# Keeping the residual feature-major in a two-block transformer kernel on one Trainium2 core

## The reference, cut to what matters

```
def rmsnorm(x, g):  xf * rsqrt(mean(xf*xf, -1) + EPS) * g
x = x + mixed @ w_out                      # block 1: three branches: gated delta rule, forget attention, stick breaking
x = x + mem_attn(rmsnorm(x, norm_xq), rmsnorm(mem, norm_mem)) @ w_mo
x = x + (silu(conv(h @ w_up)[a]) * conv(h @ w_up)[b]) @ w_down       # h = rmsnorm(x, norm_ffn)
x = x + 0.5 * rmsnorm(swiglu(rmsnorm(x, ffn1_pre)), ffn1_post)       # block 2
x = x + rmsnorm([moba attention, pooling](rmsnorm(x, mix_pre)) @ w_out_2, mix_post)
x = x + rmsnorm(xa_attn(rmsnorm(x, xa_pre), rmsnorm(mem_2, mem_g)) @ xa_wo, xa_post)
x = x + 0.5 * rmsnorm(swiglu(rmsnorm(x, ffn2_pre)), ffn2_post)
```

## Time and profile before

| | us |
|---|---|
| median of three runs | 1322.25 (1321.5 to 1328.23) |
| the profiled execution, first to last instruction | 1314.1 |
| TensorE busy | 1214.3 (92%) |
| VectorE busy | 722.1 (55%) |
| ScalarE busy | 631.5 (48%) |
| first feed-forward up projections | 503.7 to 631.2 |
| second | 700.6 to 828.1 |
| third | 1118.15 to 1245.3 |

### The profile page before, as it was taken

How to read it: one execution, slowest core, us unless ns; L and a number is a source line. 1 busy time by engine, 2 the same in 40 slices (tenths; PEclk the granted TensorE clock), 3 DMA queues, 4 the chain that set the end, 5 groups by cost and what they waited for, 6 DMA issues and landing times. The chain is left out here.

```text
span 1314.1 us, 19389 instructions
## 1 busy us (share of the span) xinstructions
PE 1214.3 (92%) x8179; PEld 1112.4 (85%) x8179; DVE 722.1 (55%) x797; ACT 631.5 (48%) x785; POOL 51.1 (4%) x81
## 2 busy tenths in 40 slices
PE   4979999999889989999999999998968987999997
PEld 4977889899888779999889999886856865999985
DVE  4855443643577546877646455445474634555543
ACT  4656334543647745566535444435453633544441
POOL 6001100110000000000000000001000000000000
PEclk9989998999999999999999999998988998999999
DMA  7533332342347334555654555554412514456550
GB/s 230 150 124 96 97 97 65 96 129 97 128 139 246 129 97 150 187 193 175 211 192 157 173 184 193 193 192 155 158 65 96 177 65 144 138 184 192 193 192 32
DMA packets 144142, 194.12 MB, mean 148 GB/s; under 512 B 6136, under 2 KB 121208, under 8 KB 144056
## 3 DMA queue, kind: packets, MB, share of 16 engines
q1 hardware_dynamic: 142856, 188.43, 44.0%
q0 software_dynamic: 1200, 4.46, 1.0%
HBM read 191.82 MB, written 1.05 MB: 147 GB/s over the span
## 5 line engine op out<-in xcount | busy, mean ns | idle before, releaser
L1469 DVE TENSOR_TENSOR wlo<-raw,whi 128x2048 fp32r<-128x2048 f32 x178 | 408.4, 2296 | 292.9 <-ACT whi L1207 292.7
L922 PE MATMUL banks<-xh,whi 128*128 128x256 f32 x1704 | 496.1, 291 | 4.6 <-DVE xl L1486 3.6
L922 PE MATMUL banks<-xl,whi 128*128 128x256 f32 x1704 | 486.1, 285 | 0.0
L922 PE MATMUL banks<-xh,wlo 128*128 128x256 f32 x1704 | 485.9, 285 | 0.0
L1207 ACT ACTIVATE whi<-raw 128x2048 fp32r<-128x2048 f32 x178 | 339.5, 1909 | 209.1 <-PE banks L948 119.3
L922 PEld LDWEIGHTS banks<-xh,whi 128*128 128x128 f32 x1704 | 331.6, 195 | 12.3 <-issue 4.8
L922 PEld LDWEIGHTS banks<-xl,whi 128*128 128x128 f32 x1704 | 331.4, 194 | 1.8 <-issue 1.7
L922 PEld LDWEIGHTS banks<-xh,wlo 128*128 128x128 f32 x1704 | 330.9, 194 | 0.0
L948 PE MATMUL banks<-whi,hh 128*128 128x512 f32 x264 | 102.7, 389 | 0.0
L948 PE MATMUL banks<-wlo,hh 128*128 128x512 f32 x264 | 102.7, 389 | 0.0
L948 PE MATMUL banks<-whi,hl 128*128 128x512 f32 x264 | 102.7, 389 | 0.0
(11 more groups left out here) (362 smaller groups left out, 1532.2 us busy)
## 6 DMA issues: line engine op xcount, KB each, us to landing
raw<-in_w_in SPq DMA_DIRECT2D x40, 1024.0 KB, 5.3
raw<-in_w_up SPq DMA_DIRECT2D x22, 1024.0 KB, 5.1
raw<-in_ffn_w_gate SPq DMA_DIRECT2D x22, 1024.0 KB, 5.3
raw<-in_ffn_w_up SPq DMA_DIRECT2D x22, 1024.0 KB, 5.3
raw<-in_ffn_w_down SPq DMA_DIRECT2D x22, 1024.0 KB, 4.9
raw<-in_w_down SPq DMA_DIRECT2D x11, 1024.0 KB, 4.9
raw<-in_w_out SPq DMA_DIRECT2D x8, 1024.0 KB, 4.8
raw<-in_xa_wkv SPq DMA_DIRECT2D x8, 1024.0 KB, 5.1
```

Of the source, the lines that this page charges most:

```text
L922: ins = pe.matmul(o, a[:, k, cols_], v[:, k, :], start=(k == 0 and i == 0), stop=(k == KD - 1 and i == 2))
L1469: dve.tensor_tensor(wlo[c % RING][:, :], raw[c % RING][:, :], whi[c % RING][:, :], ALU.subtract).then_inc(dve_done, 1)
```

## The change

The residual is kept feature-major, as `xT` (eight k tiles of 128 features by 256 tokens). The projections `w_out`, `w_mo`, `w_down`, `ffn1_w_down_2`, `w_out_2` and `xa_wo_2` become kinds A and O, with the weights stationary, and their result is added to `xT` without a transpose (`radd`); only the last one, `ffn2_w_down_2`, stays kind R, and `xT` is transposed back for it (`bt`, `btc`). The norms of x take `xT * g` as the projection's input (`xg`, `xlo`) and multiply by the token's factor at the projection's output: `rcopy` and `cu` on VectorE, `fg` and `fr` in the second and third feed-forward parts, a per-partition scale for values. `norm_ffn` alone scales its input (`SCALED`, `xn`). The factor comes from squares (`rsq`), their sum (`sqa`), a matmul with ones (`ssum`) and Ln and Exp (`srn`). The norms after sublayers become `psq`, `pf`, `psa`, `pt`, `pu`. PSUM banks are handed out in a ring of four or eight. The order changes too: x is loaded after the first weights, queries precede memory keys, `xa_k(3)` moves ahead of `w_up`, and `xa_v(1)` moves ahead of `w_out_2`.

```diff
+SCALED = ("norm_ffn",)
...
+    def down(name, K, x, evac, norm):
+        for p in range(4):
+            for k0 in range(0, K, KD):
+                k1 = min(k0 + KD, K)
+                out.append(dict(kind="A", srcs=[((0, 256), kpn(w[name][P * k0:P * k1, 256 * p:256 * p + 256]))], x=x,
+                                k0=k0, k1=k1, K=K, p=p, evac=evac if k1 == K else None, norm=norm, name=name))
...
-    rows("w_out", 4, "x", "resid")
+                            i=i, evac="gated"))
+    down("w_out", KD, "mix", "resid", "norm_xq")
     for i in range(2):
-        cols("w_mkv", 256 * i, "m1", (i,), "copy", to="mk", i=i)
+        cols("w_mq", 256 * i, "x", "rcopy", to="mq", i=i)
     for i in range(2):
-        cols("w_mq", 256 * i, "x", (i,), "copy", to="mq", i=i)
+        cols("w_mkv", 256 * i, "m1", "copy", to="mk", i=i)
...
+    xa_k(3)
...
+    down("w_down", KF, "h0", "resid", "ffn1_pre_g_2")
+    ffn(1, "ffn1_w_gate_2", "ffn1_w_up_2", 0)
+    down("ffn1_w_down_2", KF, "h1", "post", "mix_pre_g_2")
...
-    rows("w_out_2", 4, "y5", "post")
+        cols(win, 1536 + 256 * i, "x", "rcopy", to="pin", i=i)
     xa_v(1)
+    down("w_out_2", KD, "y5", "post", "xa_pre_g_2")
     for i in range(4):
-        cols("xa_wq_2", 256 * i, "x", (i % 2,), "copy", to="xq", i=i)
-    rows("xa_wo_2", 4, "y5", "post")
-    ffn(2, "ffn2_w_gate_2", "ffn2_w_up_2", "ffn2_w_down_2", 0)
+        cols("xa_wq_2", 256 * i, "x", "rcopy", to="xq", i=i)
+    down("xa_wo_2", KD, "y5", "post", "ffn2_pre_g_2")
+    ffn(2, "ffn2_w_gate_2", "ffn2_w_up_2", 0)
+    rows("ffn2_w_down_2", KF // 2, "h2", "last")
...
+            pl.add("dve", "cu", c)
...
+    def x_part(name, p):
+        if name not in SCALED:
+            pl.add("act", "xg", name, p)
+            pl.add("dve", "xlo", name, p)
+        pl.add("act", "rsq", name, p)
+        if p:
+            pl.add("dve", "sqa", name, p)
...
+    def stats(name):
+        b = pl.next_banks()
+        group[name] = b[0]
+        pl.take(("ssum", name), b, ("srn", name))
+        pl.add("pe", "ssum", name)
+        pl.add("act", "srn", name)
+    def columns(name):
+        b = pl.next_banks()
+        group["rcol", name] = b[0]
+        pl.take(("rcol", name), b, ("rcolc", name))
+        pl.add("pe", "rcol", name)
+        pl.add("dve", "rcolc", name)
+    def scale_x(name):
+        for p in range(4):
+            pl.add("dve", "xn", name, p)
+            pl.add("act", "xnh", name, p)
+            pl.add("dve", "xnl", name, p)
+    def post_x(post, name):
+        stats(post)
+        for p in range(4):
+            pl.add("dve", "pt", post, p)
+            pl.add("dve", "pu", post, p)
+            pl.add("act", "xg", name, p)
+            if p:
+                pl.add("dve", "xlo", name, p - 1)
+                pl.add("act", "rsq", name, p - 1)
+        pl.add("dve", "xlo", name, 3)
+        pl.add("act", "rsq", name, 3)
+        for p in range(1, 4):
+            pl.add("dve", "sqa", name, p)
+        x_new(name)
...
+    pl.add("act", "hi", 0)
+    for j in range(4):
+        pl.add("pe", "xt", j)
+        pl.add("act", "xg0", j)
+        pl.add("dve", "xl0", j)
+        if j == 0:
+            pl.add("dve", "lo", 0)
+    for j in range(4):
+        pl.add("act", "rsq", "norm_mix", j)
+        if j:
+            pl.add("dve", "sqa", "norm_mix", j)
     split(1)
-    norm("norm_mix")
+    for j in range(4):
+        pl.add("act", "xc", j)
+    pl.bank_limit, pl.bank_at = 4, 0
+    x_new("norm_mix")
+    ready["x"] = ("xl0",)
     pl.add("pool", "consts2")
+    side.append([[lambda: stats("norm_mix")], [lambda: columns("norm_mix")]])
...
+    side.append([[lambda: stats("norm_ffn")], [lambda: scale_x("norm_ffn")]])
...
+    side.append([[lambda: post_x("ffn1_post_g_2", "mix_pre_g_2")]])
...
         pl.add("dve", "pl_win", g)
         hook()
+    mm(c)
+    mm(c + 1)
+    c += 2
...
+    post_x("mix_post_g_2", "xa_pre_g_2")
+    side.append([[], [lambda: stats("xa_pre_g_2")]])
...
+    side.append([[lambda: back(0)], [lambda: back(1)], [lambda: back(2)], [lambda: back(3)]])
...
+            def ssum(name):
+                if name in LAST_POST:
+                    after(pe, "psa", LAST_POST[name])
+                else:
+                    after(pe, "sqa", name, 3)
+                for step in plan.bank_wait[("ssum", name)]:
+                    after(pe, *step)
+                o, q = bank(plan.bank_of[name])[:, 0:T], square_sum(name)
+                pe.matmul(o, ones[:, :], q[:, 0:T], start=True, stop=False)
+                pe.matmul(o, ones[:, :], q[:, T:2 * T], start=False, stop=True).then_inc(pe_done, 1)
...
+                elif ch["kind"] == "A" and fresh:
+                    for k in range(4 * part, 4 * part + 4):
+                        if k % 2 == 0:
+                            after(pe, *fresh, k // 2)
+                        for m in range(2):
+                            for i, (a, v) in enumerate(((wh, Xh), (wh, Xl), (wl, Xh))):
+                                ins = pe.matmul(bank(b[0])[:, m * T:(m + 1) * T], a[:, k, m * P:(m + 1) * P], v[:, k, :],
+                                                start=(k == 0 and m == 0 and i == 0), stop=(k == KD - 1 and i == 2),
+                                                skip_group_check=True)
+                elif ch["kind"] == "A":
+                    k0, k1, K = ch["k0"], ch["k1"], ch["K"]
+                    for k in range(k0, k1):
+                        for i, (a, v) in enumerate(((wh, Xh), (wh, Xl), (wl, Xh))):
+                            ins = pe.matmul(bank(b[0])[:, part * T:(part + 1) * T], a[:, k - k0, part * P:(part + 1) * P], v[:, k, :],
+                                            start=(k == 0 and i == 0 and (part == 0 or K == KD)), stop=(k == K - 1 and i == 2),
+                                            skip_group_check=K > KD)
...
+            def rsq(name, p):
+                if name == "norm_mix":
+                    src = bank(4 + p)
+                    act.wait_ge(dve_done, at("xl0", p))
+                else:
+                    src = flat(xT[:, 2 * p:2 * p + 2, :])
+                    if name in POST_OF:
+                        act.wait_ge(dve_done, at("pu", POST_OF[name], p))
+                    else:
+                        act.wait_ge(dve_done, at("radd", EVAC[name, p], p))
+                if p > 2:
+                    act.wait_ge(dve_done, at("sqa", name, p - 2))
+                act.activation(squares(name, p), src, ACT.Square).then_inc(act_done, 1)
...
+            def srn(name):
+                act.wait_ge(pe_done, at("ssum", name))
+                act.wait_ge(pool_done, at("consts"))
+                o = rnP if name in LAST_POST else rnB
+                link(act.activation(o[:, :], bank(plan.bank_of[name])[:, 0:T], ACT.Ln, bias=eps, scale=1.0 / D))
+                act.activation(o[:, :], o[:, :], ACT.Exp, scale=-0.5).then_inc(act_done, 1)
...
+            def xn(name, p):
+                dve.wait_ge(act_done, at("srn", name))
+                for k in range(2):
+                    kt = 2 * p + k
+                    ins = dve.scalar_tensor_tensor(fT[:, kt, :], xT[:, kt, :], pcolumn(name, kt), rnB[:, :], ALU.mult, ALU.mult)
+                ins.then_inc(dve_done, 1)
+            def xnl(name, p):
+                dve.wait_ge(act_done, at("xnh", name, p))
+                dve.tensor_tensor(xl[:, 2 * p:2 * p + 2, :], fT[:, 2 * p:2 * p + 2, :], xh[:, 2 * p:2 * p + 2, :],
+                                  ALU.subtract).then_inc(dve_done, 1)
...
+            def rcopy(c):
+                ch = chunks[c]
+                dve.wait_ge(pe_done, at("mm", c, 1))
+                dve.wait_ge(act_done, at("srn", plan.norm_of[c]))
+                if ch["to"] == "gate" and ch["i"] == 0:
+                    dve.wait_ge(pool_done, at("consts2"))
+                dve.tensor_tensor(TO[ch["to"]][:, 2 * ch["i"]:2 * ch["i"] + 2, :], pair_of(c), every_pair(rnB), ALU.mult).then_inc(dve_done, 1)
...
+            def pf(c):
+                ch = chunks[c]
+                post = POST_OF[ch["norm"]]
+                dve.wait_ge(act_done, at("psq", c))
+                for k in range(2):
+                    kt = 2 * ch["p"] + k
+                    ins = dve.tensor_scalar(fT[:, kt, :], bank(ch["banks"][0])[:, k * T:(k + 1) * T], pcolumn(post, kt),
+                                            POST_HALF[post], ALU.mult, ALU.mult)
+                ins.then_inc(dve_done, 1)
+            def psa(c):
+                dve.wait_ge(act_done, at("psq", c))
+                dve.tensor_tensor(SQA[:, :], SQA[:, :], SQ[chunks[c]["p"] % 2][:, :], ALU.add).then_inc(dve_done, 1)
+            def pt(post, p):
+                dve.wait_ge(act_done, at("srn", post))
+                f = fT[:, 2 * p:2 * p + 2, :]
+                dve.tensor_tensor(f, f, every_pair(rnP), ALU.mult).then_inc(dve_done, 1)
+            def pu(post, p):
...
+            def cu(c):
+                i = chunks[c]["i"]
```

(98 more changed lines are left out.)

503 lines of the change are left out of this document (289 added, 214 removed).

## The result

The changed kernel takes 1340.76 us in the median of four runs (1339.21 to 1341.76), the kernel before 1321.88 in four beside it (1320.27 to 1328.23). The ratio is 1.014, 95% interval 1.0113 to 1.0167: slower by 1.4%, where 1321.0 was forecast and 1336 was the end of the range.

What follows compares the result with a forecast made beforehand. TensorE, busy 92% of the span, was taken to bound the kernel, mostly matmuls at full pace. Terms from +12.1, -37.3 and +30.3 to the clock's -2.0 summed to -1.2 us on 1314.1; plus 8.1 gave 1321.0, range 1303 to 1336.

Steps and rivals of the forecast that it cites:

- The turned projections: Six projections leave kind R: 864 matmuls of 512 columns each become two of 256, +12.1 us on TensorE.
- Rival D: New chunks: loads of stationary operands do not overlap; 864 loads are 114 us, giving 1435 us; chance 0.02.
- The cover in memory attention: Memory attention has three chunks of cover instead of two: -4.0 us, bounds -4.3 and 0.
- the branch stage: Branch stage: TensorE idle under 12 us in the profile after; 5.7 us idle before.
- the mechanism at the start: Start and convolutions: VectorE's list, 6.65 us a chunk with `cu`, delays the twelve-row product; +3.3 us, bounds -3 and +9.
- What comes in their place: Work replacing the removed norms of x, in items (1) to (4): +30.3 us, bounds 24 and 38.
- item (1): norm_xq and ffn1_pre: `xlo` of the last pair comes 2.8 us after the projection, nothing waits; `ssum` costs 1.8 us.
- Item (2): `norm_ffn`, scaled at its input: 0.5 to begin, 3.6 over the chunk, 0.5 `ssum`; 4.6 us.
- Item (3): `mix_pre`: `ssum` 0.5, wait for `lo` behind VectorE's list 1.6, `ssum` and `rcol` 0.8; 2.9 us.
- Item (4): xa_pre and ffn2_pre, norms without cover: 10.5 us each, 21.0 together; bounds 8 and 13 each.
- `xa_v(1)` before `w_out_2`: -6.3: Value matmuls moved behind the last attention link fill waits before `w_out_2`: -6.3 us, bounds -9 and -2.
- The clock: Stages with idle links had 0.91 to 0.95 granted; some links close: -2.0 us, between 0 and -5.

Runs made afterwards that it cites:

- e2: Changed kernel with `lo` of the chunk after next queued behind `radd` or `pf` in projections ending in `radd` or `psq`/`pf`; 1337.14 us, ratio 1.0118.
- e10: Changed kernel, five edits: `lo` later in `w_out`/`w_mo`, convolutions, behind `xa_k(3)`; `xa_v(1)` back behind `w_out_2`; later squares before value projection; 1325.31 us, ratio 1.0045.
- e3: Changed kernel with the last square and three additions before the second block's value projection queued one link later; 1339.69 us, ratio 1.0143.
- e1: Changed kernel with the memory norm's steps queued behind the fourth chunk of `w_out` instead of between third and fourth; 1341.42 us, ratio 1.0147.
- e9: Changed kernel with spare matmuls behind `xa_wo_2`, 16 ahead of the sum of squares and 36 behind it; 1339.24 us, ratio 1.0147.
- e4: Changed kernel with the second half of the cross-attention values, `xa_v(1)`, back behind `w_out_2`; 1335.24 us, ratio 1.0113.

## Why the prediction was wrong

**Right.** The turned projections cost what was forecast: 120.0 ns a matmul in the earlier trace rows's manner. The Trainium skill, "TensorE: Matmul & The Clock Gate", section "The mechanism", was given there only by half: besides the sentence that the forecast took, it lets a load run ahead when it goes to the background weight buffer. The trace can't tell where a load goes, but it agrees that loads are hidden: 3127 matmuls with 3126 loads fill 375.26 us at 120.0 ns. Rival D falls. The cover in memory attention (27.8 us with two chunks, 29.3 with three, so 4.3 fewer than with 5.8 added), the absence of a gap before the second up projections, and the branch stage (8.4 us idle up to the output projections, before 9.1) came as forecast; so did the mechanism at the start, sized 1.6 too small.

**The step that failed** is "What comes in their place", item (1) first: "`xlo` of the last pair comes 2.8 us after the projection" ... "so nothing waits". It came after 9.3. The sum has the chain's own instructions and their hops, all of the right length, but not the order of the queue they stand in: each `mm` puts `lo` of the chunk after next ahead of the residual's addition. e2 shows it: 6.1 us in the stage, 3.6 in the median. Of the 19.8 us between the forecast and the result, e10 wins back 15.4 by moving steps alone, some 4 of them at the start, where the loss had been forecast. So most of the miss is the order of the steps, and not the work that was added. The PSUM page of the Trainium skill ("PSUM — Partial Sum Buffer", "Engine vs sequencer instructions") calls the queues of ScalarE and VectorE strict FIFO; the trace agrees, 6.7 us of delay for an instruction whose input was there.

**Mis-sized.** Item (2), `norm_ffn`: 4.6 forecast, 8.4 measured (19.97 less two chunks of 5.8). TensorE waited 1.54 us for the sum of squares, where nothing had been put, and 2.29 instead of 0.5 for the first pair; the chunk itself came near its term (3.4 more than 5.8, forecast 3.6). e2 cuts the first wait to 0.41 and yet the stage by only 0.5. The second wait is as long in e10, where the copy of `xa_k(3)` alone stands ahead of `xnh`: the same oversight in the queue of ScalarE, read in the trace and not tested. Item (3), `mix_pre`: 2.9 forecast, 9.0 measured (the stage took 30.8 where the terms gave 24.7): the wait for `lo` was 2.84 instead of 1.6, the wait for the column factor 1.8, and 12 matmuls that need 2.7 us took 4.6 behind the first wait, at 0.63 of the clock. e3 speaks for the list of VectorE as the bound there; how much of the 6.1 each of these carries is only read from the trace, and up to 1.6 of it is scatter, as the stage took 29.2 us in e1, which doesn't touch it. Item (4), the two uncovered norms: 10.5 each forecast, 11.7 (1044.26 to 1061.80) and 12.9 measured, each less a chunk of 5.8. The sum of squares, put at 0.55, took 1.1 and 2.1; of the 12.9, e9 gives 0.6 to 1.3 to the clock.

**The order.** "`xa_v(1)` before `w_out_2`: -6.3" priced the move and "(4)" the uncovered norm, each alone. By the trace, `w_out_2` ends 40.0 us behind the last attention link instead of 38.4, so the move alone gave 4.7 and not 6.3. e4 takes both back at once and gains 4.3 us in the stage and 5.5 in the median: the cover was worth more where it had been.

**The clock.** -2.0 was forecast for idle links that close; instead new idle stretches opened, with 0.80, 0.70 and 0.64 granted in the three transitions above. The mean over an execution was 0.955 to 0.959 in the ten of the changed kernel and 0.955 to 0.966 in the 45 of the kernel before, whose profiled one had 0.965.

**What remains.** e10 is 6.7 us above the kernel before in the median, 8.4 in the spans. The turned matmuls' 12.1 us are still in it, and so are the uncovered norm before the third feed-forward and the transposes back with a 1.2 us wait behind them. These are terms of the forecast, read in the trace, not taken out one by one. That all the rest gains 4 to 5 us (12.1 less 8.4 or 6.7) is arithmetic, not an experiment.

## What to carry to other kernels

A chain that sets the end of a stage has to be priced in the queue where its steps stand: write down what each engine has been given ahead of the step, and when that can run, before adding up durations. Prefetch work such as the next chunk's conversion belongs behind the residual's own steps, except where its own chunk is the next to be late; the same edit gained 6.1 us at one norm and cost 3.3 at another, at least 2.0 of it beyond the scatter. Removing a serial step and moving away the work that covered it are one edit and want one price. And a chunk covers a chain only if no step of its own, such as the copy of its result, stands in the chain's queue.
